# Slot weights of a hierarchical MoE kernel: three bf16 parts summed by TensorE in PSUM instead of by VectorE

## The reference

```python
def hierarchical_moe(z, w_group, b_group, w_router, b_router, w_gate_up, w_down):
    """z: (B, S, D). Top-1 group, then top-2 experts within that group."""
    ...
    top_w = top_p / jnp.sum(top_p, axis=-1, keepdims=True)
    global_idx = g_sel[..., None] * EXPERTS_PER_GROUP + top_i
    combine = jnp.sum(jax.nn.one_hot(global_idx, N_EXPERTS, dtype=jnp.float32) * top_w[..., None], axis=-2)
    combine = (combine * g_p[..., None]).astype(z.dtype)
    y = jnp.zeros_like(z)
    for e in range(N_EXPERTS):
        gate, up = jnp.split(z @ w_gate_up[e], 2, axis=-1)
        y = y + combine[..., e:e + 1] * ((jax.nn.silu(gate) * up) @ w_down[e])
    return y
```

## Time and profile before

| | |
|---|---|
| Median of 3 runs | 869.06 us (868.87 to 870.09) |
| The profiled execution | 868.9 us; its span is 867.1 us |
| PE busy | 851.8 us, 98% of the span |
| DVE busy | 789.0 us, 91% |
| ACT busy | 648.2 us, 75% |
| DMA | 270.70 MB, mean 312 GB/s; 426 to 433 GB/s from 455 to 825 us |
| Granted TensorE clock | 0.998 of full speed |

### The profile page before, as it was taken

One profiled execution on the slowest core, in us unless ns is written; L12 is line 12 of the kernel. 1 busy time (PEld: TensorE's weight loads), 2 busy tenths in 40 slices (PEclk: granted clock), 3 DMA queues, 4 the chain that ended last, 5 costly groups with the idle time before them and its releaser, 6 DMA issues.

```text
span 867.1 us, 14577 instructions
## 1 busy us (share of the span) xinstructions
PE 851.8 (98%) x5738; PEld 753.4 (87%) x5738; DVE 789.0 (91%) x782; ACT 648.2 (75%) x629; POOL 22.7 (3%) x30
## 2 busy tenths in 40 slices
PE   8999999999999999999999999999999999999996
PEld 7999999999889999877788888888888888888874
DVE  6368999999877786789999999999999999999996
ACT  6563425354554466578999999999999999999995
POOL 0110000000000000016000000000000000000000
PEclk9999999999999999999999999999999999999999
DMA  9952545544442449736999999999999999999971
GB/s 357 428 217 98 203 184 194 194 164 176 154 187 97 166 171 400 260 146 260 385 426 426 429 426 429 429 426 433 425 432 426 431 427 426 432 426 432 423 293 49
DMA packets 20455, 270.70 MB, mean 312 GB/s; under 512 B 2240, under 2 KB 2496, under 8 KB 4160
## 3 DMA queue, kind: packets, MB, share of 16 engines
q1 hardware_dynamic: 19856, 268.06, 75.8%
q10 hardware_dynamic: 560, 2.10, 0.6%
HBM read 269.10 MB, written 1.05 MB: 312 GB/s over the span
## 4 chain that ended last, share of the span: by engine, by line
PE 80%; DVE 13%; issue 3%; ACT 2%; DMA 1%; ACTq 0%; DVEq 0%
PE ps L1569 23%; PE ps L1583 11%; PE ps L1383 9%; PE ps L1385 9%; PE ps L1384 9%; PE ps L1554 4%; PE ps L1593 3%; DVE lo L1099 3%; DVE lo L824 3%; DVE conv L923 2%; PE ps L1667 1%; PE ps L1350 1%; PE ps L1674 1%; DVE lo_last L1099 1%; PE ps L1400 1%
## 5 line engine op out<-in xcount | busy, mean ns | idle before, releaser
L1099 DVE TENSOR_TENSOR lo<-raw,hi 128x2048 fp32r<-128x2048 f32 x142 | 319.1, 2282 | 0.3 <-ACT hi L653 0.3
L653 ACT ACTIVATE hi<-raw 128x2048 fp32r<-128x2048 f32 x141 | 264.9, 1916 | 15.7 <-PE ps L1569 15.7
L442 ACT ACTIVATE hi<-raw 128x2048 fp32r<-128x2048 f32 x62 | 118.6, 1914 | 58.5 <-PE ps L1385 37.6
L824 DVE TENSOR_TENSOR lo<-raw,hi 128x2048 fp32r<-128x2048 f32 x61 | 139.3, 2288 | 20.3 <-ACT hi L442 18.9
L1383 PE MATMUL ps<-inA,hi 128*128 128x256 f32 x544 | 155.0, 285 | 1.4 <-DVE lo L824 1.4
L1569 PE MATMUL ps<-hi,xeT 128*128 128x512 f32 x384 | 154.4, 402 | 0.2
L1385 PE MATMUL ps<-inA,lo 128*128 128x256 f32 x544 | 153.9, 283 | 0.0
L1384 PE MATMUL ps<-inA,hi 128*128 128x256 f32 x544 | 153.9, 283 | 0.0
L1569 PE MATMUL ps<-lo,xeT 128*128 128x512 f32 x384 | 150.1, 391 | 0.0
L1099 DVE TENSOR_TENSOR lo_last<-raw,hi_last 128x2048 fp32r<-128x2048 f32 x48 | 109.6, 2283 | 0.0
L1383 PEld LDWEIGHTS ps<-inA,hi 128*128 128x128 f32 x544 | 104.4, 192 | 2.4 <-DVE lo L824 2.4
(11 more groups left out here) (257 smaller groups left out, 1291.9 us busy)
## 6 DMA issues: line engine op xcount, KB each, us to landing
raw<-in_w_experts SPq DMA_DIRECT2D x96, 2048.0 KB, 11.9
raw<-in_w_dense SPq DMA_DIRECT2D x28, 2048.0 KB, 7.8
raw<-in_w_dense SPq DMA_DIRECT2D x3, 1024.0 KB, 11.5
x_sb<-in_x SPq DMA_DIRECT2D x2, 512.0 KB, 3.9
raw<-in_w_dense SPq DMA_DIRECT2D x2, 512.0 KB, 7.1
mem_sb<-in_mem SPq DMA_DIRECT2D x1, 1024.0 KB, 15.4
x_again<-in_x ACTq DMA_DIRECT2D x1, 1024.0 KB, 17.6
ffn_row<-in_rows ACTq DMA_DIRECT2D x1, 512.0 KB, 7.7
```

What stands on the lines that cost most here:

```text
L442: return nc.scalar.activation(conv_half(hi, N), raw_half(slot, h), ACT.Copy)
L653: nc.scalar.activation(expert_half(hi, N0), raw_flat(slot, k % 2), ACT.Copy).then_inc(hi_made, 1)
L824: nc.vector.tensor_tensor(conv_half(lo, N), raw_half(slot, h), conv_half(hi, N).bitcast(f32), ALU.subtract).then_inc(lo_made, 1)
L1099: nc.vector.tensor_tensor(expert_half(lo, N0), raw_flat(expert_slot(m), k % 2), expert_half(hi, N0).bitcast(f32), ALU.subtract).then_inc(l ...
```

## The change

The four products with 9 columns become twelve products with 3 columns. For each tile of positions and each expert, the part k = 0, 1, 2 of the three values is multiplied into the same three columns of G0, so that PSUM adds up the parts as well. ACT copies these three columns straight to `slot_sums` (one more instruction) and then `put` alone (256 columns, before 268). DVE's `slot_weights` is gone. The other engines' waits stay as they were; ACT now waits for a semaphore that it raises itself.

```diff
                 act.wait_ge(slotted, i + 1)
-                nc.scalar.activation(put_parts[:, r, :], G0[:, 0:PUT_AT + T], ACT.Copy).then_inc(put_made, 1)
+                nc.scalar.activation(slot_sums[:, r, :], G0[:, 0:3], ACT.Copy).then_inc(slot_sums_made, 1)
+                nc.scalar.activation(put[:, r, :], G0[:, PUT_AT:PUT_AT + T], ACT.Copy).then_inc(put_made, 1)
...
-            def slot_weights(i, par):
-
-                dve.wait_ge(put_made, i + 1)
-                nc.vector.tensor_reduce(slot_sums[:, par, :],
-                                        put_parts[:, par, 0:WEIGHT_COLS].bitcast(f32).rearrange("p (v k) -> p v k", k=3),
-                                        AX.X, ALU.add).then_inc(slot_sums_made, 1)
-
...
-                slot_weights(i, r)
...
+                    weights = comb[:, t, q, :].rearrange("p o (v k) -> p (o v) k", k=3)
                     for x in range(2):
-                        mm(G0[:, 0:WEIGHT_COLS], picked(t, x), comb[:, t, q, :].rearrange("p o k -> p (o k)"),
-                           start=(t == 0 and x == 0), stop=(t == TT - 1 and x == 1), skip_group_check=True)
+                        for k in range(3):
+                            mm(G0[:, 0:3], picked(t, x), weights[:, :, k], start=(t == 0 and x == 0 and k == 0),
+                               stop=(t == TT - 1 and x == 1 and k == 2), skip_group_check=True)
```

## The result

| | before | changed |
|---|---|---|
| Median (13 runs each, same chips) | 869.58 us (868.51 to 870.09) | 871.34 us (870.31 to 871.88) |
| Ratio | | 1.0019, 95% interval 1.0012 to 1.0026 |
| The profiled execution | 868.9 us, span 867.1 | 871.3 us, span 869.6 |

The changed kernel is slower by 1.76 us (1.0 to 2.3 by the interval). The forecast was a loss of 1.46 us by its sum, and 870.5 us from a median of 869.06; both of its ranges held 871.34, the narrow one (to 871.4) only just. The median of the kernel before is 0.52 us higher here than in the three runs that the forecast started from.

What follows compares the result with a forecast made beforehand. DVE was taken as the bound, PE 0.03 us a pair behind. Terms -0.81 + 2.93 - 0.42 - 0.24 = +1.46 us led to 870.5 us; narrow range 869.7 to 871.4, 8-in-10 range 868.9 to 872.3.

Steps and rivals of the forecast that it cites:

- Which engine sets the pace: Steady pairs: DVE sets the pace before, PE after the change; distance between blocks 29.34 us in place of 29.17.
- The blocks of pairs 2 to 15: Added small products on PE in 14 pairs, 14 x 0.21 = +2.93 us, from 2.5 to 3.1.
- PE's distance from the bound, 0.03 us a pair: PE's own waits in pairs 2 to 15 go: 14 x 0.03 = -0.42 us, between -0.3 and -0.6.
- Eight products at 0.026, 0.21 us a pair: Eight more products a pair on PE, each with its weight load, 0.21 us together, from 0.18 to 0.22.
- The start, -0.81 us: Pairs 0 and 1: ACT no longer waits for DVE's sum; -0.81 us, between -0.4 and -1.0.
- Both of its parts: Pairs 0 and 1: DVE, with PE following, 0.49 us earlier; PE's wait for `y_lo`, 0.32 us, gone.
- the first block of the loop: Sign in the profile after: this block comes about 0.8 - 0.2 = 0.6 us earlier if the start's term is right.
- ACT's new copy, 0.19 us, hidden: Added copy of three columns on ACT, 0.19 us, between 0.1 and 0.3, covered by ACT's wait for PE.
- ACT's wait for the sums, 0.23 us a pair: ACT's wait for `slot_sums`, 3.0 us in 13 pairs, 0.23 us a pair, goes.
- The register operations at nothing: PE's sequencer, six a pair in place of two: taken as hidden, at nothing; uncovered 2.9 us in 12 pairs.
- The end, -0.24 us: Pair 15: PE comes later, but the first 0.24 us of the delay were spare before DVE's product: -0.24 us.
- the chances of 0.52 and 0.43: Chances given to no change (0.52) and slower (0.43); faster means below 867.3 us, slower above 870.8.

Runs made afterwards that it cites:

- one part: Against the changed kernel, only the first of three bf16 parts kept: four products a pair; 867.85 us beside 869.01 for the kernel before, ratio 0.9987.
- PE's half only: Against the kernel before, eight more products of 3 columns a pair into unused columns, DVE's sum kept; 871.20 us beside 869.01, ratio 1.0024.
- fixed address: Against the changed kernel, routing weights of pairs 2 and 3 used for all loop pairs, so no register operations there; ratio 1.0018 to the kernel before.

## Why the prediction was right, point by point

- **Which engine sets the pace.** Right. DVE set it at 29.16, PE was close behind, and with PE's products PE sets it. The distance was forecast at 29.34 and is 29.352. The blocks of pairs 2 to 15 cost 14 x 0.211 = 2.95 us, forecast 2.93.
- **PE's distance from the bound, 0.03 us a pair.** A little too much: one part shows PE at 29.141, so it was 29.162 - 29.141 = 0.021. The 0.03 was the difference of two steps that are given to 0.01 us. Over the 14 pairs that is 0.29 in place of 0.42 us. This is the larger part of the 0.1 us by which the sum (+1.46) missed the stages (+1.56).
- **Eight products at 0.026, 0.21 us a pair.** Right: 0.0264 each, 0.211. The step does not depend on 3 or 9 columns (29.141 and 29.138 us a pair with four products).
- **The start, -0.81 us.** Right in size, -0.82, and in its cause: it goes with ACT's wait, since it is missing where DVE's sum is still waited for (PE's half only) and 0.67 of it is there where DVE's sum is only not waited for. Both of its parts came as forecast. DVE's `pick` of pair 1 starts 433.94 us behind the block of pair 0 before (436.80 less 402.86) and 433.45 in the changed kernel (437.18 less 403.73), 0.49 us earlier, and PE's products that follow `lo_last` gain the same 0.49. The extra steps at `y_lo` of the earlier trace rows are gone in the changed kernel:

```profile
444.04 0.40 PE L1562 MATMUL ps<-lo,xeT 128*128 128x512 f32 x1
444.27 0.40 PE L1586 MATMUL ps<-y_hi,put_parts 128*128 128x512 f32 x1
444.51 0.40 PE L1586 MATMUL ps<-y_lo,put_parts 128*128 128x512 f32 x1
```

  From the last `lo` to `y_lo` they are 0.47 us, where they were 0.78.

- My text then said that the first block of the loop would come 0.6 us earlier. It came 0.82 earlier, counted from pair 0: the products added in pairs 0 and 1 had already been paid in the 0.81, and I had taken off 0.2 a second time. They cost nothing there, since the stage takes 50.64 us with 4, 8 and 12 products a pair. The sum did not use that number.
- **ACT's new copy, 0.19 us, hidden.** The size was wrong, the cover right. It is much cheaper than the row I had taken, 0.05 us from start to start:

```profile
573.54 0.16 ACT L751 ACTIVATE slot_sums<-ps 128x3 f32<-128x3 f32 x1
573.59 0.39 ACT L752 ACTIVATE put_parts<-ps 128x256 fp32r<-128x256 f32 x1
574.41 1.92 ACT L653 ACTIVATE hi<-raw 128x2048 fp32r<-128x2048 f32 x1 [0.43 <-PE ps L1562]
```

  ACT's wait for PE behind it has grown from 0.28 to 0.43 us, since PE's release comes later.
- **ACT's wait for the sums, 0.23 us a pair.** Misread, without effect on the sum: the 3.0 us of the earlier trace rows hold the 0.7 of pair 15, and the other twelve pairs have 0.19 each.
- **The register operations at nothing.** Right, by the fixed address.
- **The end, -0.24 us.** Right. One part, with PE's block as before, has 35.38 where the kernel before has 35.64: -0.26. The changed kernel adds 0.21 for its own block and comes to 35.58. The way was right too: DVE now waits for PE, with 0.09 us from the end of the fold (842.77 + 1.00) to DVE's start, where 0.1 was allowed for the signal, so that 0.34 less 0.09 = 0.25 us were spare (the timelines of PE and of DVE in pair 15):

```profile
842.77 1.00 PE L1669 MATMUL ps<-cst,gu_sb 128*128 128x64 f32 x8
...
843.86 0.69 DVE L1254 TENSOR_TENSOR silu_sb<-silu_sb,ps 128x512 f32<-128x512 f32 x1 [0.22 <-issue]
```

- **Faster, same, slower.** The forecast lay just inside the bound of 0.2%, 1.7 us, and the measured loss lies on it: 1.76 us by the medians, 0.19% by the ratio, with an interval from 0.12 to 0.26%. That there is a loss is clear of noise. Its size was right to 0.3 us, and which side of the line it falls on was not to be known from the profile, as the chances of 0.52 and 0.43 said. That the time itself came to within 0.1 us of the narrow range's top is owed to the median of the kernel before, which moved by 0.52 us, and to no term of the sum.

## What to carry to other kernels

Where two engines are full in a steady loop, work moved from one to the other is worth at most their distance (here 0.02 us a pair), and it costs what it adds on the other side, less that distance: DVE's 0.07 us were bought with 0.21 us of PE. Read the distance between the same instruction of successive turns on each engine, and take the sum of the steps of each without its waits, before moving anything. If a third engine is idle, the work can go there, as GpSimd's sums did for 1.4 us here, but look at what its neighbours do at that moment: beside DVE's operations on SBUF the same addition held up the last pair by 4 us. And judge changes of this size by stages behind a common point, not by spans.

## What the runs showed of the hardware that I had not expected

- A GpSimd addition of three columns took 0.9 to 2.2 us beside DVE's operations with two SBUF inputs, and 5.4 us when three more of them followed without a gap; its second addition, beside DVE's `xeT` with an input from PSUM, took 0.19 us. In the pairs 2 to 14 nothing waited for it.
- ACT's copy of 3 columns from PSUM let the next copy start after 0.05 us, where a copy of 128 columns took 0.19 from start to start.
- Each small product cost 0.026 to 0.027 us, its load of 128 columns (95 ns by its row) with it, from 4 to 24 products a pair.
